# First expert's products by pairs of weight rows, and the last prompt tile finished by TensorE and ScalarE, in a two-layer decoder step

## The reference

```python
def moe_swiglu(x, router, router_b, w1, w3, w2):
    logits = einsum('btd,de->bte', x, router) + router_b
    top_p, top_i = lax.top_k(softmax(logits), 2)
    top_p = top_p / top_p.sum(-1, keepdims=True)
    ...
    for e in range(8):      # w1[e], w3[e]: 1024 x 1408, w2[e]: 1408 x 1024
        h = silu(x @ w1[e]) * (x @ w3[e])
        y = y + gates[..., e:e + 1] * (h @ w2[e])

x = layer_norm(ALPHA * x + mix(x))
x = layer_norm(ALPHA * x + ffn(x))     # (v - mean) * rsqrt(var + eps) * g + b
```

## Time and profile before

| | us |
|---|---|
| median of 3 runs | 1006.69 |
| lowest, highest | 1002.21, 1008.4 |
| the profiled execution | 1004.63 |
| its span | 1002.8 |
| TensorE busy in it | 986.8 |
| expert 0's first product to the last prompt store's issue | 640.76 to 998.91 |

### The profile page before, as it was taken

One profiled execution on the slowest core, in us unless ns is written; L12 is line 12 of the kernel. 1 busy time (PEld: TensorE's weight loads), 2 busy tenths in 40 slices (PEclk: granted clock), 3 DMA queues, 4 the chain that ended last, 5 costly groups with the idle time before them and its releaser, 6 DMA issues.

```text
span 1002.8 us, 23772 instructions
## 1 busy us (share of the span) xinstructions
PE 986.8 (98%) x10688; PEld 789.7 (79%) x10688; DVE 504.6 (50%) x1032; ACT 193.0 (19%) x414; POOL 81.8 (8%) x105
## 2 busy tenths in 40 slices
PE   9999999999999999999999999999999999999995
PEld 6897877999999999998988779556666767667533
DVE  6888894764666654269878975430101201011135
ACT  1333333221111000044333241400000000000001
POOL 1110021600000000000000200230000020000020
PEclk9999999999999999999999999999999999999998
DMA  9427349214443155201233378899999999999982
GB/s 356 148 90 240 117 151 368 91 74 180 168 168 128 74 191 222 108 29 57 86 103 132 120 307 333 332 331 379 402 415 398 422 391 412 425 421 423 422 334 83
DMA packets 37498, 241.43 MB, mean 241 GB/s; under 512 B 5008, under 2 KB 8144, under 8 KB 17680
## 3 DMA queue, kind: packets, MB, share of 16 engines
q1 hardware_dynamic: 27280, 216.69, 55.3%
q0 software_dynamic: 6432, 19.43, 5.4%
q10 hardware_dynamic: 3680, 3.74, 1.2%
HBM read 228.60 MB, written 13.07 MB: 241 GB/s over the span
## 4 chain that ended last, share of the span: by engine, by line
PE 91%; DVE 4%; DMA 3%; ACT 1%; issue 1%; SPq 0%; DVEq 0%
PE ps L773 69%; PE ps L1378 15%; PE ps L1486 6%; DMA up_slots<-in_moe_w 3%; PE ps L776 1%; PE ps L1315 1%; DVE overlay L2506 0%; DVE small L2459 0%; ACT up_slots L1835 0%; ACT x L1835 0%; DVE tables L3096 0%; DVE x L2266 0%; ACT overlay L1835 0%; DVE overlay L2261 0%; DVE overlay L2464 0%
## 5 line engine op out<-in xcount | busy, mean ns | idle before, releaser
L773 PE MATMUL ps<-up_slots,mix_or_moe 128*32 128x352 f32 (+2 forms) x3248 | 238.8, 451 | 0.6 <-DMA up_slots<-in_moe_w 0.4
L773 PEld LDWEIGHTS ps<-up_slots,mix_or_moe 128*32 128x32 f32 (+2 forms) x3248 | 135.5, 111 | 96.3 <-issue 9.3
L773 PE MATMUL ps<-x,up_slots 128*128 128x144 f32 (+3 forms) x832 | 152.3, 336 | 0.0
L773 PEld LDWEIGHTS ps<-x,up_slots 128*128 128x128 f32 x832 | 124.7, 190 | 25.1 <-issue 8.8
L773 PE MATMUL ps<-overlay,tables 128*32 128x256 f32 (+4 forms) x1992 | 121.5, 375 | 0.0
L773 PEld LDWEIGHTS ps<-overlay,tables 128*32 128x32 f32 (+2 forms) x1992 | 91.6, 113 | 26.6 <-issue 2.4
L3135 DVE TENSOR_TENSOR mix_or_moe<-mix_or_moe,ps 128x352 f32<-128x352 f32 x24 | 11.2, 518 | 174.0 <-PE ps L773 174.0
L1378 PE MATMUL ps<-overlay,up_slots 128*128 128x144 f32 x704 | 91.7, 286 | 0.6 <-DVE overlay L2911 0.3
L1378 PEld LDWEIGHTS ps<-overlay,up_slots 128*128 128x128 f32 x704 | 88.3, 190 | 1.1 <-issue 0.8
L773 PE MATMUL ps<-up_slots 128*128 128x144 f32 (+2 forms) x768 | 87.1, 282 | 1.2 <-DVE up_slots L2540 1.0
L773 PEld LDWEIGHTS ps<-up_slots 128*128 128x128 f32 (+2 forms) x768 | 79.5, 186 | 5.3 <-DVE up_slots L2540 1.9
(11 more groups left out here) (379 smaller groups left out, 1010.5 us busy)
## 6 DMA issues: line engine op xcount, KB each, us to landing
up_slots<-in_moe_w SPq DMA_DIRECT2D x64, 1408.0 KB, 24.9
overlay<-in_moe_w SPq DMA_DIRECT2D x21, 1536.0 KB, 26.7
up_slots<-in_ffn_w SPq DMA_DIRECT2D x30, 1024.0 KB, 6.9
up_slots<-in_w_in SPq DMA_DIRECT2D x27, 1024.0 KB, 5.1
up_slots<-in_w_out SPq DMA_DIRECT2D x8, 1024.0 KB, 7.3
overlay<-in_moe_w SPq DMA_DIRECT2D x7, 1024.0 KB, 26.4
mix_or_moe<-in_states POOLq DMA_DIRECT2D x6, 512.0 KB, 7.3
expert_tokens<-in_shape_tables POOLq DMA_DIRECT2D x8, 384.0 KB, 7.6
```

Source lines behind the costliest of these rows:

```text
L773: return pe.matmul(o, lhsT, rhs, start=start, stop=stop)
```

## The change

Five edits in one:

1. `first_up` goes by pairs of k-rows: k-rows 0 and 1 of groups 0, 1, 2, then 2 and 3, and so on. The 24 products are the same.
2. In both layers two instructions of VectorE (an addition of 128x8, L2323, and a copy of 128x288, L2324) move from the end of `gate_rows` to the head of `gate_maxima`, behind `operands(0)` and `operands(1)`.
3. Of prompt tile 1, VectorE computes only (x - mean) * g, into a buffer of its own. TensorE adds the shift row b (identity times b) and this buffer times a diagonal matrix of 1/deviation in two banks of 512 columns, and ScalarE copies them out.
4. The samples are written ahead of tile 0's second pass; the order of the stores is samples, tile 1, tile 0.
5. The two semaphores `small_zeroed` and `places_done` go; VectorE's own chain takes their place.

```diff
@@ SP, the last stores
             sp.wait_ge(S["y_rows"], 1)
+            sp.dma_start(out["y_sample"], ZLAST).then_inc(S["y_stored"], 16)
+            sp.wait_ge(S["y_last"], 4)
+            sp.dma_start(yp[1], XTK[:, 1]).then_inc(S["y_stored"], 16)
+            sp.wait_ge(S["y_rows"], 2)
             sp.dma_start(yp[0], XTK[:, 0]).then_inc(S["y_stored"], 16)
-            sp.wait_ge(S["y_rows"], 2)
-            sp.dma_start(out["y_sample"], ZLAST).then_inc(S["y_stored"], 16)
-            sp.wait_ge(S["y_rows"], 3)
-            sp.dma_start(yp[1], XTK[:, 1]).then_inc(S["y_stored"], 16)
@@ TensorE
             def first_up():
-                for k0 in (0, KH):
+                for k0 in range(0, KT, 2):
                     for g in range(NG):
                         if k0 == 0:
                             pe.wait_ge(*((S["first_xe"], g + 1) if g < 2 else (S["xe_done"], 1)))
-                        for k in range(k0, k0 + KH):
+                        for k in range(k0, k0 + 2):
...
+                def shift_part(i):
+                    mm(PS[:, i, 0:512], ident, LNROWS[:, 1, 512 * i:512 * i + 512], True, False)
+                def scaled_part(i):
+                    mm(PS[:, i, 0:512], DIAG, YSCALED[:, 512 * i:512 * i + 512], False, True).then_inc(S["y_ps"], 1)
...
+                shift_part(0)
+                sample_sum(0, ZSUM)
+                shift_part(1)
+                pe.wait_ge(S["z_xc"], 3)
+                pe.wait_ge(S["y_diag"], 1)
+                scaled_part(0)
+                sample_sum(1, ZSQ)
+                scaled_part(1)
@@ ScalarE, last_norm
+                evict(0)
                 act.wait_ge(S["zs_ps"], 2)
                 f(ZSD[:, 2:3], PS[:, 7, CO + 1:CO + 2], ACT.Sqrt, bias=LN_EPS).then_inc(S["z_sd"], 1)
+                evict(1)
@@ VectorE
                     link(v.memset(rtmp[:, SEQ:T:DSEQ], NEG))
+
+                def gate_maxima():
                     link(tt(N0S[:, 48:56], rlf[:, SEQ:T:DSEQ], M0[:, l, :], AD))
                     link(cp(rlf, rli))
-
-                def gate_maxima():
...
-                    v.memset(SM[:, 0:270], 0.0).then_inc(S["small_zeroed"], 1)
+                    link(v.memset(SM[:, 0:270], 0.0))
...
-            stt(PB[0:NS, 2], PS[0:NS, 0, 16:24], CAP - 1.0, slot0[0:NS, 2], MN, AD).then_inc(S["places_done"], 1)
-            v.wait_ge(S["places_done"], 1)
+            link(stt(PB[0:NS, 2], PS[0:NS, 0, 16:24], CAP - 1.0, slot0[0:NS, 2], MN, AD))
@@ VectorE, last_norm
-                for t in range(2):
-                    v.wait_ge(S["z_sq"], t + 1)
-                    link(stt(XTK[:, t], XTK[:, t], ZMEAN[:, t:t + 1], LNROWS[:, 0], AD, M))
-                    if t == 0:
-                        v.wait_ge(S["zs_ps"], 1)
-                        sig(ts(ZMEAN[:, 2:3], PS[:, 7, CO:CO + 1], -1.0, None, M), S["z_xc"], 3)
+                stt(YSCALED, XTK[:, 1], ZMEAN[:, 1:2], LNROWS[:, 0], AD, M).then_inc(S["z_xc"], 1)
+                v.wait_ge(S["zs_ps"], 1)
+                sig(ts(ZMEAN[:, 2:3], PS[:, 7, CO:CO + 1], -1.0, None, M), S["z_xc"], 4)
                 v.wait_ge(S["z_sd"], 2)
                 link(v.reciprocal(ZSD[:, 0:2], ZSD[:, 0:2]))
-                stt(XTK[:, 0], XTK[:, 0], ZSD[:, 0:1], LNROWS[:, 1], M, AD).then_inc(S["y_rows"], 1)
+                ts(DIAG, ident, ZSD[:, 1:2], None, M).then_inc(S["y_diag"], 1)
+                link(stt(XTK[:, 0], XTK[:, 0], ZMEAN[:, 0:1], LNROWS[:, 0], AD, M))
...
-                stt(XTK[:, 1], XTK[:, 1], ZSD[:, 1:2], LNROWS[:, 1], M, AD).then_inc(S["y_rows"], 1)
+                stt(XTK[:, 0], XTK[:, 0], ZSD[:, 0:1], LNROWS[:, 1], M, AD).then_inc(S["y_rows"], 1)
```

More of the change, by code:

```diff
@@ L95 @@
 x_sum ln_mean_ps ln_sq ln_fold ln_var_ps ln_xc ln_sd ln_xn z_xc dve_chain
-y_stored lgp_ps lgp_done logits_ps first_xe xtk_ps xtk_done flag_ready lg_ready xg_zeroed small_zeroed sel_done pos_ps count_ps places_done oh_ready oh_ps
+y_stored lgp_ps lgp_done logits_ps first_xe xtk_ps xtk_done flag_ready lg_ready xg_zeroed sel_done pos_ps count_ps oh_ready oh_ps
 idx_ready gate_exp rows_sent xgt_in_0 xgt_in_1 xe_done d_x d_x_ps u1_step u3_step u3_last ht_done dn_step
-moe_s moe_h x_vector y_ev y_last y_sent gh_ready gh_ps gt_ready comb_ps base_ready sample_in z_total zs_ps glo_in_0 glo_in_1 glo_in_2 ln_room dl_step ghi_in_0 ghi_in_1 ghi_in_2 ln_rows_in z_sq z_sd y_rows gate_row d_up
+moe_s moe_h x_vector y_ev y_last y_sent gh_ready gh_ps gt_ready comb_ps base_ready sample_in z_total zs_ps glo_in_0 glo_in_1 glo_in_2 ln_room dl_step ghi_in_0 ghi_in_1 ghi_in_2 ln_rows_in z_sq z_sd y_diag y_ps y_rows gate_row d_up
 d_dn d_ye d_gate_ps
@@ L352, in decoder_kernel @@
         LNROWS, LNLAST = cut(MB, 5696, 2, D), cut(MB, 5696 + 2 * D, 2, CO)
+        DIAG, YSCALED = GLO[:, 0, 0:P], GLO[:, 1]
         ZLAST = OV[:, 8 * D + 2 * CO:8 * D + 3 * CO]
@@ L1739, in sample_sums, with sample_sum @@
             def sample_sums():
-                for i, col in enumerate((ZSUM, ZSQ)):
+                def shift_part(i):
+                    mm(PS[:, i, 0:512], ident, LNROWS[:, 1, 512 * i:512 * i + 512], True, False)
+                def scaled_part(i):
+                    mm(PS[:, i, 0:512], DIAG, YSCALED[:, 512 * i:512 * i + 512], False, True).then_inc(S["y_ps"], 1)
+                def sample_sum(i, col):
                     pe.wait_ge(S["z_total"], i + 1)
                     mm(PS[:, 7, CO + i:CO + i + 1], tb("tokmean"), col[:, 2:3]).then_inc(S["zs_ps"], 1)
+                pe.wait_ge(S["ln_rows_in"], 32 * (1 + NCH))
+                pe.wait_ge(S["z_xc"], 2)
+                shift_part(0)
[6 more added lines that the diff above has]
+                scaled_part(1)
             with pe.If(sparse):
@@ L2118, in last_norm, with evict @@
                     f(ZSD[:, t:t + 1], ZSQ[:, t:t + 1], ACT.Sqrt, scale=1.0 / D, bias=LN_EPS).then_inc(S["z_sd"], 1)
-                act.wait_ge(S["z_xc"], 3)
+                act.wait_ge(S["z_xc"], 4)
                 f(GHI[:, 2, 0:CO], ZLAST, ACT.Square, bias=ZMEAN[:, 2:3], accum_out=ZSQ[:, 2:3]).then_inc(S["z_total"], 1)
+                def evict(i):
+                    act.wait_ge(S["y_ps"], i + 1)
+                    f(XTK[:, 1, 512 * i:512 * i + 512], PS[:, i, 0:512], ACT.Copy).then_inc(S["y_last"], 1)
+                evict(0)
                 act.wait_ge(S["zs_ps"], 2)
                 f(ZSD[:, 2:3], PS[:, 7, CO + 1:CO + 2], ACT.Sqrt, bias=LN_EPS).then_inc(S["z_sd"], 1)
+                evict(1)
             with act.If(sparse):
@@ L2160, in _ @@
                 act.sem_inc(S["y_ev"], NG * (NE - 1))
+                act.sem_inc(S["y_last"], 2)
                 last_norm()
@@ L3040, in _ @@
                     scale(1, 0, 1, "ln_ffn_g")
-            v.wait_ge(S["small_zeroed"], 1)
             v.wait_ge(S["logits_ps"], 1)
```

## The result

| us | before | changed |
|---|---|---|
| median of 20 runs | 1007.04 | 1009.68 |
| lowest, highest | 1001.56, 1011.4 | 1007.75, 1013.77 |
| the profiled execution | 1004.63 | 1009.55 |
| its span | 1002.8 | 1007.8 |

The ratio is 1.0047, with a 95% interval of 1.003 to 1.0064 (it isn't the quotient of the two medians, which is 1.0026): the change makes the kernel slower by a quarter to a half of a per cent. The two profiled executions differ by 4.92 us, the medians by 2.64; why these are not the same turns out to be the main lesson of this case.

The account below looks back on a forecast made before the run. TensorE was taken to set the end, with weight transfers filling nearly the same time. 1004.63 + 8.0 stall + 1.5 half clock - 0.47 gate rows - 0.44 later wait - 0.55 tail = 1012.7 us; range of 8 in 10: 1002.5 to 1019.

Parts of the forecast that it names:

- The bound and the place: From expert 0 on TensorE sets the end; ahead of expert 1 its tokens have 1.39 us to spare, stall 8.0 us.
- Group 2's tokens in time: Expert 0: group 2's tokens, wanted after 4 products instead of 8, are ready with 1.0 us to spare, cost 0.
- The issue at 645.97: SP asks for expert 1's first weights 1.34 us behind product 6's end at 644.63, 2.58 us earlier than before.
- The first rival: At expert 1's weight issue: late signals let the scatter get through first, so not slower, 1003.2 us; chance 0.36.
- Turns by packet, 27 per us: Queues alternate by packet; beside 11 KB weight pieces the scatter keeps 27 packets per us and lands at 661.8, 9.4 later.
- the weights' packets begin 1.5 us behind their issue: Expert 1's first weight packets start moving at 647.5, an estimate with 0.45 us as its lower end.
- The read again 15.0 us: Reading back expert 1's token rows behind the scatter takes 15.0 us as before.
- The half clock: Behind the gap ahead of expert 1 TensorE may start at half clock: 1.5 us lost, at most 2.3.
- The later wait, -0.44: TensorE's 0.44 us wait ahead of expert 7's w3 goes, because the weights get ahead by the stall.
- Edit 2, -0.47: Layer 1: TensorE's 0.47 us wait for the operands goes with two VectorE steps moved; layer 0 counted as 0.
- The tail, -0.55: Last norm and stores: 0.98 us less VectorE work, less a new wait of some 0.4; bounds -1.0 to +0.5.
- I shift nothing.: The profiled execution, 2.06 us below the median of three but inside their 6.2 us spread, serves as base uncorrected.

Follow-up runs that it names:

- experiment 2: The kernel before with only the order by pairs in expert 0's w1 products, none of the other four edits: 1010.76 us, ratio 1.0034 to before.
- experiment 3: The changed kernel, but SP waits until the scatter has landed before asking for expert 1's first weights: 1006.62 us, ratio 0.9996 to before.
- experiment 5: The changed kernel with each of expert 1's four w1 pairs sent as two DMAs of one k-row, 5.5 KB pieces: 1001.86 us, ratio 0.9965 to before.
- experiment 6: The changed kernel with expert 1's first weight pair waiting for u1_step 4 (product 12) instead of 2 (product 6): 1001.84 us, ratio 0.996 to before.
- hold to step 4: Expert 1's first weight pair waits for u1_step 4, not 2: changed kernel 1001.84 us; with old tail 1003.36; kernel before 1003.97; with tile 0 finished and stored first 1004.23.
- experiment 4: The kernel before run once more, unchanged, for a second profile: 1005.45 us, ratio 0.9987 to before; the profiled execution took 1009.21.
- tile 0 first: The changed kernel with edit 4 turned round, VectorE finishing tile 0 ahead of the samples, stores tile 0, tile 1, samples: 1009.33 us, ratio 1.0036 to before.
- experiments 5 to 8: Changed kernel with smaller weight pieces, first pair held to u1_step 4, old tail, or tile 0 stored first: 1001.86, 1001.84, 1008.94, 1009.33 us; before beside them 1008.68.

## Why the prediction was right, and where its steps were off

The forecast was a stall ahead of expert 1 behind a scatter that lands late, 1012.7 us on the basis of the profiled execution; that one took 1009.55, the median is 1009.68. Experiments 2, 3, 5 and 6 show the mechanism from four sides. The total is partly luck: 8.0 us more than the profiled execution were forecast and 4.9 measured, and of the 3.1 between them 1.1 are gaps of expert 0 that were no term of the sum, while the stall, the last expert and the tail were off by -2.0, -2.2 and +1.7. By its steps:

- *The bound and the place.* Right: the only new idle time of TensorE above 1 us is ahead of expert 1, and edit 1 alone brings it.
- *Group 2's tokens in time.* Right: TensorE's 384 matmul records of expert 0 stand in one row without a gap.
- *The issue at 645.97.* It was 644.30. The step that failed is "with 1.34 the issue is at 645.97": the lateness of 1.24 and 1.34 us was taken for a property of the place, but it was one of that execution. Here SP follows product 6 (644.08 at 0.596 us a product) by 0.2 us. The 0.645 us a product was wrong too: it spread the gaps behind product 10 over all 24, and so it also put the lateness of the earlier trace rows at 1.34 where it was 1.8. Of the 1.67 us, 0.26 are the earlier start, 0.29 the product's time and 1.12 the lateness. The first rival had its basis in the same lateness; it is real, but it belongs to some executions, and the forecast should have had two values with a chance each.
- *Turns by packet, 27 per us.* Right, and this is the step that carried the forecast. The queues of the changed kernel from 646 to 648 and from 648 to 658:

```profile
q0 software_dynamic: 217, 0.78, 95.8%
q1 hardware_dynamic: 7, 0.08, 9.3%
```
```profile
q1 hardware_dynamic: 316, 3.21, 75.6%
q0 software_dynamic: 308, 1.04, 25.7%
```

  The scatter has the engines alone until the weights' first packets come, between 647.5 and 648, and then both queues move 31 packets per us each for 10 us. 325 of its packets were left at 648, and by 658 all but 17 were through. The step that failed is "the weights' packets begin 1.5 us behind their issue": here they began 3.2 to 3.7 us behind it. It is 3.0 to 3.8 us in all seven profiles with a stall, and 0.7 to 2.1 in before and the four profiles with the hold to step 4; what sets it stays open. The issue came 1.67 us ahead of the forecast and the packets some 2 us later behind it, so they began where they were forecast, at 647.5: that is luck. The landing at 660.1 for 661.8 comes of the rate, 31 per us for 27; the last 17 packets took 2.1 us and gave some of it back.

  Those last packets are where equal counts end: in experiment 4, from 653 on, 17 of the scatter's packets moved beside 266 of the weights'. The Trainium skill, *DMA: Bandwidth & Descriptors*, section *Queues, rings and completion order*, says that an engine drains a packet of some 9 to 17 descriptors from one queue before it turns to the next. I had read the trace's packets as that unit. By that rule a handful of rows can wait for a whole group of 11 KB pieces; the 17 packets in 6 us, and the gain from pieces of half the size, agree with it, but on which engine each packet ran no view here shows, so this is argued and not shown.
- *The read again 15.0 us.* It was 13.26 (660.10 to 673.36), 1.7 less. And expert 0 ended at 669.11 instead of 670.49, since two gaps in TensorE's weight loads behind 646.7 did not come back; so the tokens were late by 1.4 more. Stall 5.97 for 8.0.
- *The half clock.* The term was 1.5, the weight loads show 1.8.
- *The later wait, -0.44.* The step was mis-sized: -2.6, of which 0.9 was waiting for weights and 1.7 gaps in TensorE's own issue. I had read the matmul rows alone; PEld's show a wait whole.
- *Edit 2, -0.47.* Layer 1's wait is gone, and the product starts at 464.07 for 464.42: -0.35, of which -0.26 reaches expert 0.
- *The tail, -0.55.* Sign wrong. The compute part came, with the last store's issue 0.8 us earlier and the wait of 0.33 for 0.4 forecast. The step that failed is "Tile 1's store now goes just ahead of tile 0's, where 512 KB stood ahead before as well", which put the stores at nothing: before, the first stood 2.3 us ahead, and with the shorter way of 2.9 us it landed 0.6 behind the second's issue; now the last store takes 2.0 us longer to the span's end. Net +1.2 in the two profiles. Over all profiles the old form takes 12.3 to 12.7 us from the common start to the span's end, the changed one 13.4 to 13.9, tile 0 first 12.9. From the first large store's issue to the last landing it is 5.8 to 6.6 us in all fourteen profiles, whichever order the stores have; so 0.7 of the 1.2 is that the first large store is issued at 6.8 us behind the common start instead of 6.1, and the earlier last store doesn't help.
- *"I shift nothing."* This was the reading that mattered most. The kernel before was profiled in an execution without a stall; its runs reach from 1000.7 to 1011.4, and experiment 4 has one with 5.42 us. So part of what the change costs was in the median of before already, and the medians moved by 2.6 and 5.8 us in the two comparisons, not by the 7.8 of the stall and the clock. How many of before's runs stall isn't shown, since two were profiled. A spread of 6 us in three runs, where every stage is gapless in the profile, should have told me that the margin of 1.39 us is crossed in some of them.

## What to carry to other kernels

A transfer that is asked for earlier than needed is not free: look which small, urgent transfer is still in the queues, and at how large the pieces are that it must pass; 17 small packets beside 11 KB pieces took 6 us here, where 341 ahead of the pieces took 3. Where both ends matter, hold the large one just long enough: held by 3 us, the changed kernel was faster than before on a chip where before can stall (ratio 0.996, medians 6.8 us apart); held by 8 us it was not (0.9996). And where the runs of a kernel spread much further than its noise, take a second profile before pricing a change against the first.

## What was not expected of the hardware

- TensorE's signals come in two forms. In the prompt one VectorE is idle for 1.1 us ahead of the third transpose, in the late one 2.27 to 2.28, and then TensorE's weight loads show gaps of 0.5 to 0.8 us around 646 to 648 and of up to 1.3 around 975. All three profiles of one chip had the late form, all eight of another the prompt one. On the first the kernel before had no run above 1005.92 (from 1002.25); on the other its runs fell in two heaps (in the session of experiments 5 to 8 ten from 1001.26 to 1003.15, the other 21 from 1006.24 to 1011.2). What makes the difference stays open, and so does whether the two heaps are runs with and without the stall.
- The weights' first packets moved 0.7 to 2.1 us behind their issue in five profiles without a stall and 3.0 to 3.8 in the seven with one; what sets this no run here shows.
- With both queues full the counts of packets were equal (308 and 316 in 10 us with 11 KB pieces, 201 and 180 in 4 us with 5.5 KB pieces), and yet the scatter's last 17 packets took 6 us beside 266 of the weights'.
- The last of the three stores (512, 512 and 128 KB) landed 5.1 to 5.7 us behind its issue where all three were issued within 1.4 us, and 3.5 to 3.9 where they were spread over 2.3; from the first large one's issue it was 5.8 to 6.6 us in all.
